# A fused decoder layer: negated scores, split-product scores for two token tiles, and three selection rounds one group later

## The reference, cut to what matters

```python
score = jnp.einsum('bqhs,bqh->bqs', jax.nn.relu(logits), w_idx)     # the indexer, 4 heads
_, sel = lax.top_k(score, topk)                                     # topk = 128 keys per query
q_lat = jnp.einsum('bthd,hdc->bthc', q_a, w_uk)
s = jnp.einsum('bqhc,bqkc->bqhk', q_lat, kv_sel) * (64 ** -0.5)
p = jax.nn.softmax(s, axis=-1)                                      # over the selected keys
o_lat = jnp.einsum('bqhk,bqkc->bqhc', p, kv_sel)
y_att = jnp.einsum('bthc,hcd->bthd', o_lat, w_uv)
```

## Time and profile before

| | |
|---|---|
| median of three executions | 1014.8 us |
| profiled execution: its time, its span | 1015.58 us, 1013.8 us |
| PE busy | 994.0 us (98%) |
| DVE, ACT, POOL busy | 723.1, 500.1, 120.4 us |
| chain that ended last: PE, DVE, ACT | 80%, 15%, 2% |
| mean granted TensorE clock | 0.997 of full speed |

### The profile page before, as it was taken

One profiled execution on the slowest core, in us unless ns is written; L12 is line 12 of the kernel. 1 busy time (PEld: TensorE's weight loads), 2 busy tenths in 40 slices (PEclk: granted clock), 3 DMA queues, 4 the chain that ended last, 5 costly groups with the idle time before them and its releaser, 6 DMA issues.

```text
span 1013.8 us, 19077 instructions
## 1 busy us (share of the span) xinstructions
PE 994.0 (98%) x7048; PEld 911.8 (90%) x7048; DVE 723.1 (71%) x1331; ACT 500.1 (49%) x883; POOL 120.4 (12%) x96
## 2 busy tenths in 40 slices
PE   8999999999999999999999999999999999999996
PEld 8999999999999989699866778889999999988886
DVE  7988888888322263599999743699989889942336
ACT  6655655566221254646336732576656665812121
POOL 0000000000121252045221205310000000000000
PEclk9999999999999999999999999999999999999998
DMA  7223232323223313131110102113323232433312
GB/s 253 84 90 118 89 118 83 124 71 114 87 86 92 111 65 107 43 125 60 67 42 1 43 1 83 42 43 125 124 83 124 87 120 95 127 103 103 97 57 84
DMA packets 30849, 90.48 MB, mean 89 GB/s; under 512 B 4689, under 2 KB 5329, under 8 KB 30801
## 3 DMA queue, kind: packets, MB, share of 16 engines
q1 hardware_dynamic: 30800, 89.83, 26.7%
HBM read 87.72 MB, written 2.10 MB: 89 GB/s over the span
## 4 chain that ended last, share of the span: by engine, by line
PE 80%; DVE 15%; ACT 2%; issue 1%; DMA 1%; SPq 0%; DVEq 0%; ACTq 0%
PE ps L1255 38%; PE ps L1313 22%; PE ps L1178 9%; DVE sc L2246 3%; DVE top L2245 3%; PE ps L1450 1%; PE ps L1718 1%; DVE qk L2285 1%; PE ps L1732 1%; PE ps L1758 1%; DVE wlo L1922 1%; PE ps L1515 1%; PE ps L1363 1%; PE ps L1361 1%; DMA wraw<-in_ffn_w_up 1%
## 5 line engine op out<-in xcount | busy, mean ns | idle before, releaser
L1255 PE MATMUL ps<-tsum,whi 128*128 128x264 f32 (+1 forms) x1280 | 243.1, 282 | 0.5 <-ACT ht L815 0.5
L1255 PEld LDWEIGHTS ps<-tsum,whi 128*128 128x128 f32 x1280 | 202.5, 188 | 0.7 <-issue 0.7
L1255 PE MATMUL ps<-tsum,wlo 128*128 128x264 f32 (+1 forms) x640 | 180.6, 282 | 0.0
L1255 PE MATMUL ps<-xh,whi 128*128 128x264 f32 (+1 forms) x480 | 135.6, 282 | 0.3 <-ACT sil L815 0.3
L1255 PE MATMUL ps<-xl,whi 128*128 128x264 f32 (+1 forms) x480 | 135.7, 283 | 0.0
L1255 PE MATMUL ps<-xh,wlo 128*128 128x264 f32 (+1 forms) x480 | 135.5, 282 | 0.0
L754 ACT ACTIVATE whi<-wraw 128x1408 fp32r<-128x1408 f32 (+1 forms) x48 | 74.6, 1555 | 122.7 <-PE ps L1313 121.2
L1832 DVE TENSOR_TENSOR wlo<-wraw,whi 128x1408 fp32r<-128x1408 f32 (+1 forms) x38 | 70.1, 1844 | 85.9 <-ACT whi L754 85.9
L1313 PE MATMUL ps<-hh,whi 128*128 128x264 f32 (+1 forms) x462 | 124.3, 323 | 0.0
L1313 PE MATMUL ps<-hh,wlo 128*128 128x264 f32 (+1 forms) x462 | 123.5, 322 | 0.0
L1313 PE MATMUL ps<-hl,whi 128*128 128x264 f32 (+1 forms) x462 | 123.4, 321 | 0.0
(11 more groups left out here) (305 smaller groups left out, 1861.8 us busy)
## 6 DMA issues: line engine op xcount, KB each, us to landing
wraw<-in_ffn_w_gate SPq DMA_DIRECT2D x43, 512.0 KB, 4.0
wraw<-in_ffn_w_up SPq DMA_DIRECT2D x42, 512.0 KB, 4.3
wraw<-in_ffn_w_down SPq DMA_DIRECT2D x32, 384.0 KB, 3.2
wraw<-in_ffn_w_down SPq DMA_DIRECT2D x32, 320.0 KB, 3.5
wraw<-in_w_in SPq DMA_DIRECT2D x19, 512.0 KB, 4.3
wraw<-in_w_out SPq DMA_DIRECT2D x8, 512.0 KB, 4.4
out<-zrow SPq DMA_DIRECT2D x8, 256.0 KB, 2.0
x<-in_x SPq DMA_DIRECT2D x3, 528.0 KB, 7.3
```

Source lines behind the costliest of these rows:

```text
L1255: mm = pe.matmul(ps[:, bank, 0:(HT, HALF_SEQ)[p // 2]], w[:, k * P:(k + 1) * P], v[:, k, :], start=(first and k == 0 and n == 0), stop=(k ...
```

## The change

- `masked(k)`: the score is multiplied by minus the scale before the mask is added, and the reduction is a minimum. It writes the bias itself. L2388 and the semaphore `nmax_ready` go; `exps` waits for `s_masked` and uses scale -1.
- For tiles 3 and 4 (`SPLIT_J = 3`) `scores(k)` is a split product of three fp32r matmuls per part. The first of them (k = 16) waits for `att_split` to reach 6.
- POOL makes the parts: `split_keys_hi` (a 128x528 copy) ahead of `split_latents`, and after it `split_queries` (two copies of 128x4x256, two subtractions of the same shape) and `split_keys_lo` (a 128x528 subtraction). All stand ahead of the low parts of the gated heads. `split_queries` waits for all eight heads of `ql`.
- `LATE_AT` becomes (3, 4, 5): the three late rounds, and with the last of them the comparison L2248 and POOL's causal mask of tile 4, come one group later.
- Some tensors are placed elsewhere in SBUF: the parts of the queries in `xh`, `xl` and over `ql`, the low keys over `wuk`.

```diff
-LATE_AT = (2, 3, 4)
+LATE_AT = (3, 4, 5)
+SPLIT_J = 3
...
+        LATE_T = slice(START[SPLIT_J], END[NT - 1])
+        def query_hi(h):
+            return (xh if h < 4 else xl)[:, h % 4, :]
...
+                def split_keys_hi():
+                    pool.wait_ge(ct_ready, 1)
+                    pool.tensor_copy(ct_hi[:, :], ct[:, :]).then_inc(att_split, 1)
+                def split_keys_lo():
+                    pool.wait_ge(att_split, 1)
+                    pool.wait_ge(ql_done, ATT_H)
+                    pool.tensor_tensor(ct_lo[:, :], ct[:, :], ct_hi[:, :].bitcast(F32), ALU.subtract).then_inc(att_split, 1)
+                def split_queries():
+                    pool.wait_ge(ql_own, QL_DVE)
+                    pool.wait_ge(ql_ready, ATT_H - QL_DVE)
+                    for e, v in enumerate((xh, xl)):
+                        pool.tensor_copy(v[:, 0:4, LATE_T], ql[:, 4 * e:4 * e + 4, LATE_T]).then_inc(att_split, 1)
+                    for e, v in enumerate((xh, xl)):
+                        q = ql[:, 4 * e:4 * e + 4, LATE_T]
+                        pool.wait_ge(att_split, e + 2)
+                        pool.tensor_tensor(ql_low[:, 4 * e:4 * e + 4, LATE_T], q, v[:, 0:4, LATE_T].bitcast(F32), ALU.subtract).then_inc(att_split, 1)
                 mix_lo(N_PROJ)
+                split_keys_hi()
                 split_latents()
+                split_queries()
+                split_keys_lo()
...
-                        act.wait_ge(nmax_ready, k + 1)
+                        act.wait_ge(s_masked, k + 1)
...
-                                       bias=nmax[:, j, h:h + 1], scale=ATT_SCALE,
+                                       bias=nmax[:, j, h:h + 1], scale=-1.0,
...
+                    if j >= SPLIT_J:
+                        if k % ATT_H == 0 and j == SPLIT_J:
+                            pe.wait_ge(att_split, 6)
+                        q_h, q_l = query_hi(h)[:, START[j]:END[j]], ql_low[:, h, START[j]:END[j]]
+                        for e in range(parts):
+                            dst = ps[:, 4 + 2 * (k % 2) + e, 0:w]
+                            pe.matmul(dst, q_h, ct_hi[:, e * w:(e + 1) * w], start=True, stop=False)
+                            pe.matmul(dst, q_l, ct_hi[:, e * w:(e + 1) * w], start=False, stop=False)
+                            mm = pe.matmul(dst, q_h, ct_lo[:, e * w:(e + 1) * w], start=False, stop=True)
...
-                    dve.tensor_tensor_reduce(dst, keys(P, n, 4 + 2 * (k % 2)), msk, 1.0, -3.0e38, ALU.add, ALU.max,
-                                             smax[:, j, h:h + 1]).then_inc(s_masked, 1)
-                    dve.wait_ge(s_masked, k + 1)
-                    dve.tensor_scalar(nmax[:, j, h:h + 1], smax[:, j, h:h + 1], -ATT_SCALE, None, ALU.mult)\
-                        .then_inc(nmax_ready, 1)
+                    dve.tensor_tensor_reduce(dst, keys(P, n, 4 + 2 * (k % 2)), msk, -ATT_SCALE, 3.0e38, ALU.add, ALU.min,
+                                             nmax[:, j, h:h + 1]).then_inc(s_masked, 1)
```

More of the change, by code:

```diff
@@ L178, in build @@
             qa = sb("qa", [P, 4, T], F32, s)
-            ql = sb("ql", [P, ATT_H, T], F32, s)
+            with ExitStack() as ql_scope:
+                ql = sb("ql", [P, ATT_H, T], F32, ql_scope)
+            ql_low = sb("ql_low", [P, ATT_H, T], F32R, s)
             ct = sb("ct", [P, T], F32, s)
@@ L184, in build @@
             clo, chi = c_parts[:, :, 0:LAT], c_parts[:, :, LAT:2 * LAT]
-            wuk = sb("wuk", [P, 4, LAT], F32, s)
+            ct_hi = sb("ct_hi", [P, T], F32R, s)
+            with ExitStack() as wuk_scope:
+                ct_lo = sb("ct_lo", [P, T], F32R, wuk_scope)
+            with ExitStack() as wuk_scope:
+                wuk = sb("wuk", [P, 4, LAT], F32, wuk_scope)
+            sb("ct_lo_room", [P, T], F32, s)
             wuv = sb("wuv", [P, ATT_H, ATT_D], F32, s)
@@ L195, in build @@
             rows = sb("rows", [P, 2, T], F32, s)
-            kvg = sb("kvg", [P, LAT], F32, s)
+            with ExitStack() as kvg_scope:
+                kvg = sb("kvg", [P, LAT], F32, kvg_scope)
+            bst = sb("bst", [P, ML_H * 4, 6], F32, s)
+            mv = sb("mv", [P, ML_H * 4, 2], F32, s)
             bg = sb("bg", [P, 8], F32, s)
@@ L205, in build @@
             crms = sb("crms", [P, 2, NT], F32, s)
-            smax = sb("smax", [P, NT, ATT_H], F32, s)
             nmax = sb("nmax", [P, NT, ATT_H], F32, s)
@@ L209, in build @@
             rinv = sb("rinv", [P, NT, ATT_H], F32, s)
-            bst = sb("bst", [P, ML_H * 4, 6], F32, s)
-            mv = sb("mv", [P, ML_H * 4, 2], F32, s)
             mls = sb("mls", [P, 3, ML_H * 4], F32, s)
@@ L360, in build @@
         c_ready = sem("c_ready")
+        att_split = sem("att_split")
         ct_turned = sem("ct_turned")
@@ L404, in build @@
         s_masked = sem("s_masked")
-        nmax_ready = sem("nmax_ready")
         p_ready = sem("p_ready")
@@ L1716, in scores @@
                     w = n // parts
+                    if j >= SPLIT_J:
[7 more added lines that the diff above has]
+                            mm = pe.matmul(dst, q_h, ct_lo[:, e * w:(e + 1) * w], start=False, stop=True)
+                        mm.then_inc(s_done, 1)
+                        return
                     for e in range(parts):
```

## The result

The changed kernel takes 1018.6 us (median of 7 runs, 1018.0 to 1019.8) where the kernel before took 1015.0 beside it (1014.4 to 1016.6): a ratio of 1.0037, with an interval of 1.0027 to 1.0046. Its profiled execution took 1018.4 us, 1016.7 of them span.

A forecast was written before the change was run, and what follows sets the result against it. DVE was taken to bound attention before 563.4 us, PE behind it and after attention. Hold 5.5 + clock 1.1 - gains 3.4 = +3.2 us: profiled 1018.8, median 1018.0 us; range 1010.9 to 1020.0.

The forecast's parts named there:

- The step that decided: Norming of mLSTM head 2 on DVE, at 533.4 us: its four instructions take turns with POOL's queue, plus 5.5 us.
- rival A: Norming of head 2: DVE is not held beside POOL, only the gains stand, 1011.4 us; chance 0.27.
- Rival B: Norming of head 2: DVE waits for one subtraction, 2.4 us, then keeps its turn; 1013.8 us; chance 0.11.
- The clock: PE in groups 1 and 2, after its idle gap: falls to 1.2 GHz, costing 1.1 us (between 0 and 3).
- The gains: Attention: 2.5 us up to 563.4 us, minus 0.7 in group 5, plus 1.65 from split scores, rounded to 3.4.
- The negated minimum: 32 short DVE instructions go: 0.35 us gained in groups 0 and 1, 0.65 in groups 3 and 4.
- The round out of group 2: Group 2 loses its late round, 1.45 us on DVE and chain; the next turn stands 1.5 us earlier.
- The comparison out of group 4: Group 4 keeps one late round but loses the comparison on DVE, gaining 0.35 us.
- The round in group 5: Late round and comparison, 1.8 us more DVE work ahead of the third `weights_lo`: minus 0.7 us.
- The split product: PE scores of tiles 3 and 4: 1.4 us gained for tile 4, 0.25 for tile 3, 1.65 in all.
- C: Rival: the late round starves group 5, costing another 1 to 2 us; its chance is counted within the other cases.

The follow-up runs named there:

- e9: The kernel before with only POOL's five new instructions added, their results unused: 1022.6 us, ratio 1.0073.
- e1: The changed kernel with POOL's query and key subtractions waiting until mLSTM head 2 is normed: 1011.6 us, ratio 0.9957.
- e11: The changed kernel with head 2 normed by a scalar_tensor_tensor whose second operand, the reciprocal deviation, lies in PSUM: 1011.7 us, ratio 0.9965.
- e12: The changed kernel with an accumulator output on all sixteen norming tensor_scalar instructions: 1011.9 us, ratio 0.9965.
- e2: The changed kernel with 20 filler matmuls of 128 columns on PE where group 1 waits: 1016.4 us, ratio 1.0009.
- e3: The kernel before with the negated minimum alone: 1012.7 us, ratio 0.9978.
- e4: The kernel before with the negated minimum and the late rounds in groups 3, 4 and 5, no split scores or new POOL work: 1012.4 us, ratio 0.9967.
- e5: The changed kernel with POOL's two query subtractions cut into eight pieces of 256 columns: 1014.0 us, ratio 0.9985.

## Why the prediction was right

**The step that decided**, that L2365 of head 2 is held by POOL's new queue with the engines taking turns, is shown: by its rows, by e9 (the POOL work alone makes the loss), by e1 (moved, the hold of head 2 is gone) and by e11 and e12 (another form, it is gone). The turns fell as the prediction had them: one passes behind the copies, then one behind each query subtraction and one behind the key subtraction. Predicted 5.5 us, measured 5.1 in the traces: I had added 0.2 us for each turn that POOL gives up, which its rows don't show, and POOL's queue was 7.9 us long (530.8 to 538.7) where I had 8.3. PE's gap was put at 536.5 to 541.7 us and stood at 534.7 to 539.7, about as long. One argument for the hold was read wrongly: 0.490 us for 528 columns against 0.69 for 512 is 1.4 times as fast and not nearly twice, and the L2294 that was held in the earlier trace rows is of the slower kind. Duration doesn't tell what is held, as e11 shows.

The Trainium skill (SBUF — State Buffer, "SBUF: two separate sides") has the first to start keep the pair of ports for its whole instruction, and the trace agrees where POOL's instruction is a subtraction: 2.383 us for an instruction of 0.343. The Trainium skill (SBUF — State Buffer, "Who interferes with whom") takes tensor_scalar's form that also writes out its accumulator out of those that want the pair, and e12 agrees: 0.403 us, not held.

**Where the casts misled.** The row for rival A had a norming instruction pass beside POOL's casts almost untouched. It still passes so: the first L2412 starts at 532.60, 0.23 us before the end of the second cast, and takes 0.343. Neither trace shows a cast holding a norming instruction, so the rule of the Trainium skill that whichever starts first blocks the other is borne out here for POOL's subtractions and not for its casts. That one instruction got through a cast is no evidence about a train of them behind a subtraction. Whether a long cast would hold a train I did not try. Rival B (DVE keeps its turn) is excluded by the second to fourth durations, A by the first row of DVE's timeline.

**The clock** is the term that was mis-sized: 1.1 us put, 1.8 to 2.6 measured (2.6 in e2 against the changed kernel; 1.8 in e9, between groups 1 and 2). The fall itself was read rightly from the idle end. What failed is "DVE still hides most of it": at 1.2 GHz PE is shown busy throughout from 540 to 545 us, and DVE and ACT half of it. DVE waited for PE's scores, not the other way round (timeline of DVE, idle time before and its releaser):
```profile
542.83 0.31 DVE L2432 CUSTOM_DVE_ANT_0 qk<-ps,sc 128x144 f32<-128x144 f32 x1 [1.28 <-PE ps L1765]
545.02 0.44 DVE L2432 CUSTOM_DVE_ANT_0 sil<-ps,sc 128x272 f32<-128x272 f32 x1 [1.21 <-PE ps L1765]
```
**The gains**: 3.4 us put, 3.4 and 3.8 measured in e11 and e1 (4.4 and 4.2 in their traces up to the last `project`). By parts:
- The negated minimum was mis-sized. e3 gains 0.37, 0.33, 0.41 and 0.30 us in groups 0 to 3, three times the 0.12 us of the earlier trace rows in each, and 0.74 in group 4: 2.15 us by group 5. The sum had 0.35 for groups 0 and 1 together and 0.65 for 3 and 4, so 1.0; by its own words for groups 3 and 4 (five of 0.12 and one handover of 0.17) it should have had 0.77 there. The handover now reads so, with the next `masked` starting with the reading of the accumulator (DVE's timeline, changed kernel):
```profile
557.23 0.08 DVE L2432 DVE_READ_ACCUMULATOR2_ANT nmax<- 128x1 f32 x1
557.23 0.44 DVE L2432 CUSTOM_DVE_ANT_0 qk<-ps,sc 128x272 f32<-128x272 f32 x1
```
- The round out of group 2: 1.0 us (at the start of group 3 e4 stands at -2.12, e3 at -1.11), 1.15 put. The comparison out of group 4: 0.25 us (0.89 between them at the start of group 4, 1.14 at group 5), 0.35 put. Together with the minimum, e1 starts group 5 at -3.4 us where the sum had -2.5.
- The round in group 5: 0.7 us put, 0.5 given back in e4, 0.4 in e1. It lies where it was said to: the third `weights_lo` straight behind it, with no idle time before, and the chain goes through all of it (timeline of DVE, then the chain).
```profile
570.70 0.70 DVE L2292 MAX8 top<-sc 128x8 f32<-128x528 f32 x1
...
572.24 0.43 DVE L2295 TENSOR_SCALAR sc<-sc 128x528 f32<-128x528 f32 x1
...
572.59 0.68 DVE L2460 TENSOR_TENSOR pts<-ps,pts 128x512 fp32r<-128x512 f32 x1
```
- The split product: a tile-4 matmul takes 0.12 us on the chain, as the earlier trace rows said, and its weight loads hide (chain of the changed kernel). From group 6 to the end e1 gains 1.1 us over e4, 1.4 put.
```profile
574.42 0.51 PE ps L1798
574.92 0.12 PE ps L1759
575.05 0.12 PE ps L1760
575.17 0.12 PE ps L1761
```
C did not come: the late round cost group 5 less than its term, and the mask was not waited for.

So the net came out at +3.6 us for +3.2 put because a clock term 0.7 to 1.5 us too small was set off by a hold 0.4 too large and gains up to 0.4 too small. The mechanism was right; the closeness of the sum was partly luck.

## What to carry to other kernels

Before work is given to an idle POOL, list what DVE runs from SBUF to SBUF in the same microseconds, and count that each such instruction may wait for one whole POOL instruction, so that a short one loses most. If such a train is on the path, start POOL's work behind it (one wait; then look where the end of its queue lands, as in e1), cut POOL's work small, or give DVE a form that isn't held (here an operand in PSUM; the accumulator form escapes too, but did not keep the values). And price a PE gap twice: once for its length, and once for the work that PE does behind it at half speed; where PE's backlog at half speed is as long as DVE's, as here, nothing hides that.

## What was unexpected of the hardware

- The clock fell after a gap of 1.28 us. In e5 and in the changed kernel PE did nearly the same work before (busy for 1.28 and 1.30 us of the 3 from 533 to 536 us); in e5 it was then idle until 535.98, worked on, and still the granted clock fell to 0.50 at about 536.5 us (0.75 is its mean from 536 to 537) and stayed to about 543.3. In the changed kernel (idle from 534.74 to 539.72) it fell at about 538.5, 2 us later, and came back at about 545.3:
```profile
538.00:539.00 1.00, 0.00 (x0) 0.00 (x0) 1.00 (x2) 0.00 (x0) 0.70 (x1) 0.76 0.00 0
539.00:540.00 1.00, 0.28 (x1) 0.28 (x2) 0.97 (x6) 0.30 (x1) 0.00 (x0) 0.50 0.00 0
...
545.00:546.00 1.00, 1.00 (x7) 0.70 (x7) 0.73 (x3) 0.22 (x1) 0.70 (x1) 0.82 0.00 0
546.00:547.00 1.00, 1.00 (x11) 1.00 (x9) 0.40 (x3) 0.84 (x2) 0.57 (x1) 1.00 0.00 0
```
  Both low stretches last 6.8 us. In the kernel before, PE was busy 2.42 of the same 3 us, and the clock stayed whole. Why the smaller gap was followed by the fall sooner stays open. e5's spread of 3.5 us between runs goes with its mean granted clock, which is on record for each: 0.994 in the four slowest (1014.8 to 1015.9 us), 0.996 in the two fastest (1012.3 and 1012.5), 0.995 between. So the low stretch seems to be shorter or absent in some executions; only one was traced, and the kernel before has 0.995 in some of its own slower runs, so this is not shown.
- Each norming instruction moves 128 columns in 0.343 us, with the factor from SBUF or from PSUM alike, but only the first form is held.
